# The last gate's second weight slab, moved from ahead of a mixture of experts into its middle

## The reference, cut to what matters

```
for i in range(2):
    x = _layernorm(ALPHA * x + mixer(x), ...)
    f = swiglu(x) if i == 0 else moe(x)
    e = sigmoid(x @ w_ple_gate[i]) * (p[i] @ w_ple_proj[i])
    x = _layernorm(ALPHA * x + f + e, ...)
```

## Time and profile before

| | |
|---|---|
| median of 3 runs | 2643.22 us (2635.3 to 2649.78) |
| profiled execution, span from first to last instruction | 2640.7 us |
| TensorE busy | 2556.6 us (97%) |
| DMA queue of SP | 587.74 MB |
| chain that ended last | PE 80%, DMA 15%, of that 14% on expert weights |
| expert units' products on VectorE | 1793.7 to 2617.6 us |

### The profile page before, as it was taken

One profiled execution on the slowest core, in us unless ns is written; L12 is line 12 of the kernel. 1 busy time (PEld: TensorE's weight loads), 2 busy tenths in 40 slices (PEclk: granted clock), 3 DMA queues, 4 the chain that ended last, 5 costly groups with the idle time before them and its releaser, 6 DMA issues.

```text
span 2640.7 us, 74266 instructions
## 1 busy us (share of the span) xinstructions
PE 2556.6 (97%) x34014; PEld 2161.4 (82%) x34014; DVE 963.8 (36%) x1799; ACT 362.6 (14%) x836; POOL 42.7 (2%) x74
## 2 busy tenths in 40 slices
PE   8999999989999999999999999998999999999998
PEld 8966778877698477875984778758999999999997
DVE  5663454633477723244666232441000000000002
ACT  1001241211100023311000233110000000000000
POOL 0000000000100000000000000010000000000000
PEclk9999999999999999999999999999999999999999
DMA  6444233004444543325435433387999999999996
GB/s 256 158 137 186 104 137 116 4 27 149 150 172 149 185 165 132 132 112 202 165 112 203 148 131 132 112 279 305 426 427 427 426 426 426 427 426 426 426 425 257
DMA packets 58054, 607.77 MB, mean 230 GB/s; under 512 B 7364, under 2 KB 7492, under 8 KB 12352
## 3 DMA queue, kind: packets, MB, share of 16 engines
q1 hardware_dynamic: 52272, 587.74, 55.8%
q0 software_dynamic: 5648, 18.07, 2.3%
HBM read 599.69 MB, written 6.09 MB: 229 GB/s over the span
## 4 chain that ended last, share of the span: by engine, by line
PE 80%; DMA 15%; DVE 2%; issue 1%; ACT 1%; SPq 0%; POOL 0%; DVEq 0%; ACTq 0%; POOLq 0%
PE bank L313 22%; PE bank L469 16%; DMA slot<-in_experts 14%; PE bank L2616 11%; PE bank L496 7%; PE bank L2629 6%; PE bank L323 5%; PE bank L1652 3%; PE bank L1218 3%; PE bank L1638 1%; PE bank L946 1%; DMA arena<-token_rows,arena 1%; PE bank L1239 1%; PE bank L2021 1%; PE bank L1311 0%
## 5 line engine op out<-in xcount | busy, mean ns | idle before, releaser
L2616 PE MATMUL bank<-arena,slot 128*64 128x84 f32 x14336 | 546.8, 237 | 19.2 <-DMA slot<-in_experts 12.1
L2616 PEld LDWEIGHTS bank<-arena,slot 128*64 128x64 f32 x14336 | 530.5, 138 | 31.0 <-issue 21.3
L313 PE MATMUL bank<-h_cm,slot 128*128 128x256 f32 (+2 forms) x2032 | 448.3, 382 | 1.2 <-ACT h_cm L356 0.6
L313 PEld LDWEIGHTS bank<-h_cm,slot 128*128 128x128 f32 (+2 forms) x2032 | 383.7, 190 | 64.0 <-issue 9.7
L2808 DVE TENSOR_TENSOR ff<-ff,bank 128x168 f32<-128x168 f32 x112 | 36.9, 329 | 654.6 <-PE bank L2616 651.4
L2629 PE MATMUL bank<-ff,arena 128*64 128x84 f32 x5376 | 211.7, 237 | 4.7 <-issue 4.4
L2629 PEld LDWEIGHTS bank<-ff,arena 128*64 128x64 f32 x5376 | 200.9, 137 | 10.2 <-issue 8.3
L469 PE MATMUL bank<-arena 128*128 128x128 f32 x1584 | 187.8, 275 | 1.1 <-DVE arena L559 1.1
L469 PEld LDWEIGHTS bank<-arena 128*128 128x128 f32 x1584 | 182.2, 192 | 1.3 <-DVE arena L559 1.3
L323 PE MATMUL bank<-slot,h_cm 128*128 128x512 f32 (+1 forms) x320 | 135.0, 579 | 1.4 <-ACT h_cm L356 1.2
L313 PE MATMUL bank<-arena,slot 128*128 128x256 f32 x608 | 132.8, 380 | 0.0
(11 more groups left out here) (441 smaller groups left out, 2564.0 us busy)
## 6 DMA issues: line engine op xcount, KB each, us to landing
slot<-in_experts SPq DMA_DIRECT2D x112, 2048.0 KB, 21.3
arena<-in_experts SPq DMA_DIRECT2D x84, 1024.0 KB, 17.0
slot<-in_ffn SPq DMA_DIRECT2D x22, 2048.0 KB, 8.3
h_cm<-in_experts SPq DMA_DIRECT2D x28, 1024.0 KB, 16.9
slot<-in_ffn SPq DMA_DIRECT2D x22, 1024.0 KB, 5.0
slot<-in_dense SPq DMA_DIRECT2D x11, 2048.0 KB, 7.7
slot<-in_dqk SPq DMA_DIRECT2D x8, 2048.0 KB, 8.3
slot<-in_g SPq DMA_DIRECT2D x8, 2048.0 KB, 8.2
```

Source lines behind the costliest of these rows:

```text
L313: ins = pe.matmul(ps[0:m, j * S:(j + 1) * S], w[:, k * width + c0:k * width + c0 + m], rhs[:, k, :], start=k == 0, stop=k == ks - 1)
L2616: ins = pe.matmul(bank[64 * c:64 * c + 64, m * PLACES:(m + 1) * PLACES], weights[:, c0:c0 + 64], CURRENT[:, k, :], start=k == 0, stop=k == ...
```

## The change

The second gate slab leaves `stream`. It is loaded early into a place of its own (`LATE_GATE`, the columns of `arena` that `CHOSEN` takes in the eighth expert), ahead of the load of `bdiff_1`, and multiplied between the fourth and the fifth expert, in the banks 6 and 7 that the turned sums use. `h_cm` must live until then, so the fourth down place becomes `x_tm`. Its part of `ALPHA * x` is written to `E_TM` ahead of the experts, and the load waits for that (`x_taken`). The second half of the projection is kept in `LATE_PROJECTED`. Router, `projection(1)` and `ranks` stand ahead of the first slab; the queue rows stand behind three eighths of its first tile. In `dve_router` the Exp is no longer waited for ahead of `ranks`, and the passes and softmax weights stand behind `PICK`. Several pairs of semaphores become one with stages (`kk_stages`, `gn_stages`, `lat_stages`, `top_stages`); the order of work is the same there.

```diff
@@ stream @@
-                slabs("plegate_1")
+                stream.append((("plegate_1", 0), dram["plegate_1"][0], dram["plegate_1"].shape[2]))
@@ places @@
-        DOWN_RING = (arena[:, 18432:20480], arena[:, 16384:18432], arena[:, 2048:4096], h_cm[:, :, :].rearrange("p k s -> p (k s)"))
+        DOWN_RING = (arena[:, 18432:20480], arena[:, 16384:18432], arena[:, 2048:4096], x_tm[:, :, :].rearrange("p t d -> p (t d)"))
+        LATE_GATE = arena[:, 22528:22528 + 4 * D]
+        LATE_PAIR = 1
-        UP_RING = [slot[(first_load["experts"] + i) % SLOTS][:, 0:4096] for i in (0, 2, 1, 3)]
+        UP_RING = [slot[(first_load["experts"] + i) % SLOTS][:, 0:4096] for i in range(RING)]
@@ pe_extras, layer 1 @@
+            router()
+            w = slab(pe, ("pleproj_1", 0))
+            product_tm(pe, ("pp", 1, 1, 0), next_bank(), w, 1024, 512, 512, PLE_CM, 2, 0)
...
+            product_tm(pe, ("pp", 1, 1, 1), next_bank(), w, 1024, 512, 512, PLE_CM, 2, 1)
+            released(("pleproj_1", 0), ("pp", 1, 1, 1))
+            ranks()
+            w = slab(pe, ("plegate_1", 0))
+            bank = next_bank()
+            product_tm(pe, ("pg", 1, 0, 0), bank, w, 512, 0, 512, h_cm[:, 0:3, :], 3, 0, stop=False)
+            pe.wait_ge(named("pick_ready"), 1)
+            filled(pe_queue_rows(pe, fill(pe, ("queue",), next_bank())), ("queue",))
+            product_tm(pe, ("pg", 1, 0, 0), bank, w[:, 3 * 512:], 512, 0, 512, h_cm[:, 3:KD, :], KD - 3, 0, start=False)
+            product_tm(pe, ("pg", 1, 0, 1), next_bank(), w, 512, 0, 512, h_cm, KD, 1)
@@ act_extras @@
+            if l == 1:
+                act.wait_ge(named("top_stages"), 1)
+                act.activation(RC[4], RC[3], ACT.Exp).then_inc(named("top_stages"), 1)
+                for t in range(T):
...
+                        ins = act.copy(LATE_PROJECTED[t][q], ps[:, q * S:(q + 1) * S])
@@ dve_extras @@
+            if l == 1:
+                v.tensor_scalar(E_TM[:, :, 512:D], x_tm[:, :, 512:D], ALPHA, None, ALU.mult).then_inc(named("x_taken"), 1)
@@ dve_router @@
-            v.tensor_tensor(RC[3], RC[1], RC[0], ALU.subtract).then_inc(named("top_two"), 1)
-            dve.wait_ge(named("top_exp"), 1)
             v.tensor_tensor(RT[4], RT[0], RT[1], ALU.add).then_inc(named("routed"), 1)
+            v.tensor_tensor(RC[3], RC[1], RC[0], ALU.subtract).then_inc(named("top_stages"), 1)
...
+            ch.step(v.tensor_scalar(PLACE, PLACE, -1.0, None, ALU.add))
+            dve_pick()
@@ new functions @@
+        def pe_late_gate(pe):
+            pe.wait_ge(named("late_loaded"), 16)
+            for t in range(T):
+                pe.wait_ge(sums_ready[t], 2 * LATE_PAIR + 2)
+                for k in range(KD):
+                    ins = pe.matmul(PS[6 + t][:, :], h_cm[:, k, t * P:(t + 1) * P], LATE_GATE[:, k * 512:(k + 1) * 512],
+                                    start=k == 0, stop=k == KD - 1)
+                ins.then_inc(named("late_gate"), 1)
+        def act_late_gate(act):
+            act.wait_ge(named("late_gate"), T)
+            for t in range(T):
+                act.activation(LATE_SIGMOID[:, t, :, :].rearrange("p q s -> p (q s)"), PS[6 + t][:, :], ACT.Sigmoid
+                               ).then_inc(named("late_read"), 1)
...
+        def dve_late_gate(dve):
...
+                    v.tensor_tensor(part, part, LATE_PROJECTED[t][q], ALU.mult).then_inc(done, 1)
...
+                    v.tensor_tensor(part, part, LATE_SIGMOID[:, t, q, :], ALU.add).then_inc(done, 1)
@@ pe_experts @@
                         with pe.If((i < 1) & (pair > 0)):
+                            pe.wait_ge(named("late_read"), pair * 2)
                             pe_moe_turn(pe, p, pair * 2 - 1)
...
+                    with pe.If((pair > LATE_PAIR - 1) & (pair < LATE_PAIR + 1) & (p < 1)):
+                        pe_late_gate(pe)
@@ pool_experts @@
+                pool.wait_ge(named("late_added"), 4 * T)
@@ sp_experts @@
+                load_up(1, 1)
                 load_down(2, 2)
...
                 load_up(2, 2)
                 if freed:
+                    sp.wait_ge(named("x_taken"), 1)
+                    sp.wait_ge(named("tokens_stored"), 16 * (T + 1))
                     sp.wait_ge(*freed[3])
                 load_up(3, 3)
@@ SP queue @@
+                if key == ("bdiff_1", 0):
+                    sp.wait_ge(named("diff_weights"), 4 * DEPTH_2)
+                    sp.dma_start(LATE_GATE, dram["plegate_1"][1]).then_inc(named("late_loaded"), 16)
```

More of the change, by code:

```diff
@@ L2415, in router @@
                     for k in range(KD):
+                        if t == 0 and k % 2 == 0:
+                            drained(pe, (("turn", 2 * l + 1), k // 2))
                         ins = pe.matmul(ps[:, t * 8:(t + 1) * 8], h_cm[:, k, t * P:(t + 1) * P], ROUTER[:, k * 8:(k + 1) * 8],
@@ L2431, in pe_extras @@
             pe_layernorm(pe, 2 * l)
[L2432 to L2449, removed]
+            if l == 0:
+                for s in range(2):
+                    if s:
+                        projection(1)
+                        released((f"pleproj_{l}", 0), ("pp", l, 1, 1))
+                    w = slab(pe, (f"plegate_{l}", s))
+                    for t in range(T):
+                        product_tm(pe, ("pg", l, s, t), next_bank(), w, 512, 0, 512, h_cm, KD, t,
+                                   turned=("turn", 2 * l + 1) if s == t == 0 else None)
+                    released((f"plegate_{l}", s), ("pg", l, s, 1))
+                return
@@ L2473, in dve_extras @@
                 dve_router(dve, ch)
-            for s in range(2):
+            for s in range(2 - l):
                 for t in range(T):
@@ L2502, in dve_router @@
                     src = RT[3]
-            v.tensor_tensor(RC[3], RC[1], RC[0], ALU.subtract).then_inc(named("top_two"), 1)
-            dve.wait_ge(named("top_exp"), 1)
             v.tensor_tensor(RT[4], RT[0], RT[1], ALU.add).then_inc(named("routed"), 1)
+            v.tensor_tensor(RC[3], RC[1], RC[0], ALU.subtract).then_inc(named("top_stages"), 1)
+            ch.step(v.tensor_tensor(HOTW, HOTS, times(const("order", 8), 4), ALU.mult))
+            ch.step(v.tensor_reduce(ORD, HOTW, AX, ALU.add))
+            ch.step(v.tensor_scalar(FAR, ORD, 2.0, None, ALU.is_ge))
             dve.wait_ge(named("routed"), 1)
+            ps = full(dve, ("rank",))
+            ch.add(v.tensor_tensor(PLACE, ps[:, 0:16].rearrange("p (t e) -> p t e", t=T), RT[4], ALU.mult))
+            free(v.tensor_copy(QUEUED, ps[:, 16:24]), ("rank",))
+            ch.fence()
+            ch.step(v.tensor_scalar(PLACE, PLACE, -1.0, None, ALU.add))
+            dve_pick()
+            drained(dve, ("rank",))
+            ch.step(v.tensor_reduce(LONGEST, QUEUED, AX, ALU.max))
+            for i in range(MAX_PASSES - 1):
+                ch.add(v.tensor_scalar(OVER[:, i:i + 1], LONGEST, float(PLACES * (i + 1)), None, ALU.is_gt))
+            ch.fence()
+            ch.step(v.tensor_reduce(LONGEST, OVER, AX, ALU.add))
+            v.tensor_scalar(PASSES, LONGEST, 1.0, None, ALU.add).then_inc(named("passes_known"), 1)
+            dve.wait_ge(named("top_stages"), 2)
             ch.step(v.tensor_scalar(RC[5], RC[4], 1.0, None, ALU.add))
@@ L2512, in dve_router @@
             ch.step(v.tensor_tensor(COMB, RT[2], RT[3], ALU.add))
[L2513 to L2528, removed]
             dve.wait_ge(named("pick_ready"), 1)
@@ L2567, in dve_chosen @@
             v, done = nc.vector, named("chosen_added")
+            dve.wait_ge(named("late_added"), 4 * T)
             dve.wait_ge(named("rows_gathered"), p * 64 + 64)
@@ L2756, in act_experts @@
                             unit(i, j)
+                    if e == 2 * LATE_PAIR + 1:
+                        with act.If(p < 1):
+                            act_late_gate(act)
                     moe_down(act, p, e, 0, act.copy)
@@ L2815, in dve_experts @@
                         moe_sums(dve, p, e - 1, 1, v.tensor_copy)
+                    if e == 2 * LATE_PAIR + 2:
+                        with dve.If(p < 1):
+                            dve_late_gate(dve)
                     with dve.Fori(1, U_EXPERT // 2 - 1) as i:
```

77 lines of the change are left out of this document (50 added, 27 removed).

## The result

The changed kernel takes 2882.16 us (median of four runs, 2874.97 to 2888.66); beside it on the same chip the kernel before takes 2639.26 (2634.55 to 2649.78). The ratio is 1.0915 [1.0893, 1.0937]: 243 us slower, where the prediction was 8 us faster and its range ended at 2648. The profiled execution spans 2886.6 us.

The account below looks back on a forecast made before the run. TensorE was taken to set the pace early, the loads from the fourth expert on. Span 2640.7 - 11.1 (earlier cast) + 2.5 (loads' hole) = 2632.1; with the median 2.5 us above the span, 2635, range 2626 to 2648.

Parts of the forecast that it names:

- the middle: Between fourth and fifth expert: late gate's 14.0 us of products plus 2.0 of fetch stall lose 2.5 us on the loads.
- The 6.2 us of more branches would cost 1: New `If` in the expert loop, passed each round: three more fetch stalls, 6.2 us on TensorE, would cost 1 us.
- the dearest case: Late-gate pause not won back and half clock also taking the gain ahead of the experts: +12.5 us, 2656.
- rival A: Experts: the late gate's pause isn't won back, all 16 us stay; +4.9 us, 2648. Chance 0.12.
- The front: Router to queue rows, ahead of the experts: cast of the queue rows 11.1 us earlier, moving the first unit's start.
- the bound was 3.5: Cast of the queue rows only 3.5 us earlier if the clock stays at half from router to queue rows.
- Rival B: Half clock from the router on eats the gain ahead of the experts: -3.5 + 2.5 = -1 us, 2642. Chance 0.12.
- The gathers: Ahead of the first unit: overlap with up 3 and down 3 stays, no gain; up to 5 us if it went.
- The late gate: Between fourth and fifth expert: 16 products of 128x512 take 14.0 us on TensorE.
- Entry stall: At the late gate's entry on TensorE: 2.0 us added for entering a stretch of code for the first time.
- Queue silent: SP queue around the late gate: next load issue waits 23.0 us instead of 7.
- rival C: More than the sum: gathers meet less of the 3 MB, or loads' hole is closed; -13 to -16 us. Chance 0.16.

Follow-up runs that it names:

- a_pad40: The changed kernel with 40 TensorE instructions (waits already met) put ahead of the expert loop, nothing else: 2631.27 us, 0.9961 of before.
- a_pad40_gate8th: a_pad40 with only one of eight k-steps of the late gate, leaving out seven eighths of that sum: 2626.86 us, 0.9954 of before.

## Why the prediction was wrong

**The step that failed** is the costing of code that is moved, in the middle: "Entering a stretch of code for the first time cost 2.05 us", and of the new `If`, "The 6.2 us of more branches would cost 1". Instruction fetch entered the sum only as single stalls of 2.05 us, one for each branch. Nothing was reckoned for *where* the expert loop comes to lie. The slab's 64 instructions leave the stretch ahead of the loop, the loop moves down by 65, crosses a border of the 256-instruction blocks, and is fetched anew every second pass. No rival had this mechanism, and no bound held it: the dearest case, within rival A, ends at 2656.

The rows for it were there. Rows 8 show a gap under "issue" in the middle of a run of equal products, and the page before counts 106 instruction packets, about one for each block of the program: the loop was resident. That said it had a size and a place that could be lost. How near the limit it lay could not be read from the trace, only counted in the program: 1609 instructions lie within 7 blocks if they begin up to 183 behind a border (7 x 256 - 1609), and before began 42 behind.

The Trainium skill bears on it in the section that the prediction drew on, "Runtime: NRT & Kernel Launch", Instruction fetch mechanics: TensorE's instruction memory is given there as 128 KiB, 2048 instructions, refilled in 16 KiB blocks of 256. The packets agree in size (16.4 KB). By that figure alone, eight blocks should hold the loop after as well; the runs show that seven hold and eight do not.

**The front.** Cast of the queue rows 11.1 us earlier: in the changed kernel it is 1752.41 against 1758.21 with everything ahead 5.36 later, 11.2 earlier net. In a_pad40 (cast at 1750.59, all ahead 1.9 later) it is 9.5, since the clock at half already caught the router (5.34 us against 3.71); the bound was 3.5. Rival B, all of the front eaten, did not happen.

**The gathers.** "The overlap stays; I take no gain" was off by the 7 us from 27.2 to 20. The prediction bounded this at 5, by the 3 MB behind the gathers. The overlap with them did stay: they are asked for 12.8 us behind the first gather in a_pad40 and 12.5 in before, and cost 1 us in a_pad40. What changed is ahead of the gathers: up 2, asked for 3.7 us before the first of them in before, was in no term. So the first up product, forecast near 1775.5, came at 1772.20 in a_pad40, 14.3 earlier than before and 16.2 net of what ran late ahead.

**The late gate.** 14.0 us of products, measured 13.97. Entry stall 2.0, measured none. Queue silent for 23.0, measured 20.5. The end lost 2.5, measured 3.2 against before's trace and 3.4 against a_pad40_gate8th's. The 6.2 us of more stalls at the `If` did not come. The experts behind at 100.9 each, measured 100.7. Rival A, the pause stays whole, is refuted: with 16 us of it a_pad40 would be near 2643 (2626.9 + 16).

**The sum.** Without the reloads the kernel takes 2631.3, where 2635 was predicted; the 251 us are one omitted term. That the rest came so near is in part luck, for the missed gain of the gathers was offset by small losses beyond the terms. From before's trace to a_pad40's the span changed by +1.9 (everything ahead, later in this execution), -9.5 (the cast, forecast -11.1), -6.7 (the gathers, forecast 0), +3.2 (the experts, forecast +2.5) and +0.8 (behind the last unit, forecast 0), together -10.3, where -8.6 was forecast. In its mechanism this is nearer to rival C, in which the gathers meet less.

**The version that beats both** is a_pad40: the change, with 40 instructions that do nothing ahead of the loop. It is 0.4% under before and 251 us, the reloads, under the change.

## What to carry to other kernels

A loop that is resident in an engine's instruction memory has a place as well as a length: any edit ahead of it, even one that only takes instructions away, can push it over one more block, and here that cost 9%. Look at the instruction queue's packets in the page against the program's size, and at idle time under "issue" in the loop; if packets exceed the blocks of the program, shift the loop with met waits before judging the edit by its time. And when small indirect transfers stand on the path, look at what is asked for just ahead of them as well as behind.

## What the hardware showed that was not expected

A loop of 1609 TensorE instructions in 7 blocks of 256 is fetched once (106 packets); in 8 blocks it is fetched again and again (241 and 224). In the changed kernel that is nine packets for each reload, at every second pass, for 17 us a time. The two nested loops count apart: with only the outer one over the border, the reload comes once for each new pass of it, three times, for 13 to 14 us each. With the stalls the granted clock fell too (0.88 over 100 us where it was 1.00). And one load of 2 MB asked for 3.7 us ahead of eight gathers of 344 KB, with 3 MB more behind them, about doubled their time to land: 9.9 to 15.1 us against 4.6 to 7.7.
